# Experts' results stored from the sync engine's queue of weight loads instead of from ScalarE

## What is computed

```
def expert_block(args):
    tok_b, e = args
    xb = xpad[tok_b]
    h = jax.nn.silu(xb @ w_gate[e]) * (xb @ w_up[e])
    return h @ w_down[e]
out = out.reshape(rows, d) * buf_wt[:, None].astype(out.dtype)
y = jnp.zeros((t + 1, d), out.dtype).at[buf_tok].add(out)[:t]
```

## Time and profile before

| what | value |
|---|---|
| median of 3 runs | 1728.08 us (1727.17 to 1729.11) |
| profiled execution, its own time | 1736.61 us |
| its span in the profile | 1734.5 us |
| mean granted TensorE clock | 0.922 of 2.4 GHz |
| TensorE busy | 1468.1 us (85%) |
| ScalarE busy | 486.5 us (28%) |
| VectorE busy | 705.7 us (41%) |
| transfers | 336.88 MB |

### The profile page before, as it was taken

The page is one execution under the profiler, slowest core; times in us unless marked ns, Lnnn a source line. Parts: engine busy times, 40 slices in busy tenths (PEclk is TensorE's granted clock), DMA queues, the critical chain, the costliest instruction groups (busy, mean ns, idle before and its releaser), DMA issues.

```text
span 1734.5 us, 17917 instructions
## 1 busy us (share of the span) xinstructions
PE 1468.1 (85%) x6858; PEld 1003.7 (58%) x6858; DVE 705.7 (41%) x1297; ACT 486.5 (28%) x723; POOL 37.6 (2%) x73
## 2 busy tenths in 40 slices
PE   6999979966867767997572699998899999999976
PEld 5787766432322322333220588877788888888865
DVE  4576656101010102010003575644526666666645
ACT  5543440100000000000002522232434444444532
POOL 1000000000000000000002001000000000000000
PEclk9998998988988989998786799998999999999988
DMA  9646444996877973498774555321122121212101
GB/s 354 274 149 232 170 147 193 387 406 255 335 311 309 403 303 147 183 419 329 305 308 145 204 202 199 148 88 70 49 98 93 53 98 49 97 58 89 49 1 61
DMA packets 48139, 336.88 MB, mean 194 GB/s; under 512 B 3600, under 2 KB 3728, under 8 KB 17424
## 3 DMA queue, kind: packets, MB, share of 16 engines
q1 hardware_dynamic: 36480, 295.77, 42.9%
q0 software_dynamic: 6624, 29.89, 4.8%
q10 hardware_dynamic: 4912, 9.51, 1.5%
HBM read 312.62 MB, written 22.54 MB: 193 GB/s over the span
## 4 chain that ended last, share of the span: by engine, by line
PE 42%; ACTq 2%; DVE 2%; ACT 2%; DMA 1%; another core or an unknown queue 1%; issue 1%; POOL 0%; DVEq 0%; POOLq 0%
PE ps L290 41%; ACTq L1018 2%; PE ps L718 1%; DMA y_scratch<-gate 1%; ACT ar L860 0%; DVE b_NL L1305 0%; DMA ar<-y_scratch,rt 0%; DVE ar L1297 0%; DVE hres L1788 0%; ACT b_NH L869 0%; PE ps L296 0%; DVE ar L1971 0%; ACT ar L1085 0%; DVE ar L1256 0%
## 5 line engine op out<-in xcount | busy, mean ns | idle before, releaser
L290 PE MATMUL ps<-ring,ar 128*64 128x512 f32 x800 | 256.5, 636 | 82.3 <-ACT ar L1007 62.3
L290 PE MATMUL ps<-ar 128*64 128x512 f32 (+5 forms) x798 | 240.8, 501 | 38.8 <-ACT ar L1007 20.2
L290 PE MATMUL ps<-b_NH,b_WH 128*128 128x512 f32 x704 | 187.0, 401 | 9.7 <-DVE b_NL L1305 5.0
L290 PEld LDWEIGHTS ps<-ring,ar 128*64 128x64 f32 x800 | 77.9, 147 | 198.8 <-issue 129.0
L290 PE MATMUL ps<-b_NH,b_WL 128*128 128x512 f32 x704 | 181.6, 394 | 0.0
L1238 DVE TENSOR_TENSOR b_WL<-ring,b_WH 128x1024 fp32r<-128x1024 f32 x112 | 136.7, 1221 | 96.9 <-ACT b_WH L812 96.9
L290 PE MATMUL ps<-b_NL,b_WH 128*128 128x512 f32 x704 | 173.8, 390 | 0.0
L290 PEld LDWEIGHTS ps<-ar 128*64 128x64 f32 (+3 forms) x798 | 98.5, 167 | 127.8 <-issue 97.2
L812 ACT ACTIVATE b_WH<-ring 128x1024 fp32r<-128x1024 f32 x112 | 118.1, 1055 | 163.0 <-PE ps L290 159.8
L290 PE MATMUL ps<-spare,ar 128*64 128x512 f32 x416 | 135.2, 638 | 23.6 <-ACT ar L1007 15.1
L290 PEld LDWEIGHTS ps<-b_NH,b_WH 128*128 128x128 f32 x704 | 130.7, 191 | 38.0 <-ACT b_NH L869 10.0
(11 more groups left out here) (269 smaller groups left out, 1888.6 us busy)
## 6 DMA issues: line engine op xcount, KB each, us to landing
ring<-in_wts_dram SPq DMA_DIRECT2D x84, 2048.0 KB, 13.3
ar<-in_wts_dram SPq DMA_DIRECT2D x24, 2048.0 KB, 20.9
spare<-in_wts_dram SPq DMA_DIRECT2D x24, 2048.0 KB, 21.1
ring<-in_wmod_dram SPq DMA_DIRECT2D x24, 512.0 KB, 4.8
ar<-in_wmod_dram POOLq DMA_DIRECT2D x24, 512.0 KB, 4.1
y_scratch<-gate POOLq DMA_DIRECT2D x11, 1024.0 KB, 21.4
y_scratch<-gate ACTq DMA_DIRECT2D x22, 256.0 KB
y_scratch<-ar ACTq DMA_DIRECT2D x10, 256.0 KB
```

The lines of the kernel that those rows point to most:

```text
L290: return pe.matmul(o, l, m, start=start, stop=stop, skip_group_check=True)
```

## The change

The store of each expert's rows moves from ScalarE's instruction list to SP's, and from ScalarE's DMA queue to the queue of the weight loads. SP issues it behind the load into the slot of that expert's last panel. The store of a second block moves too, behind the load into the slot of the expert's second panel; it becomes one transfer of 2 x 64 x 512, and all waits on `ty` count 16 for a block instead of 32.

```
             act.activation(ysb[n % 3], ps[:, 5, :], ACT.Copy).then_inc(S["m_y"], 1)
-            act.wait_ge(S["m_y"], n + 1)
-            act.dma_start(y_d[n * CAP:(n + 1) * CAP, :].rearrange("t (q c) -> q t c", q=2),
-                          ysb[n % 3]).then_inc(S[f"y{n % 3}"], 16)
-
-        def store_third(u):
-
-            r = NE * CAP + CAP * u
-            for hf in range(2):
-                act.dma_start(y_d[r:r + CAP, hf * 512:(hf + 1) * 512],
-                             ysb3[64 * hf:64 * hf + 64, :]).then_inc(S["ty"], 16)
...
             act.activation(ysb3, ps[:, 1, :], ACT.Copy).then_inc(S["t_y"], 1)
-            act.wait_ge(S["t_y"], u + 1)
-            store_third(u)
...
-                    act.wait_ge(S["ty"], 32 * n)
+                    act.wait_ge(S["ty"], 16 * n)
...
-                dve.wait_ge(S["ty"], 32 * u)
+                dve.wait_ge(S["ty"], 16 * u)
...
+        def store(b, y, sem):
+
+            sp.dma_start(y_d[b * CAP:(b + 1) * CAP, :].rearrange("t (q c) -> q t c", q=2), y).then_inc(S[sem], 16)
+
         for n in range(NE):
             for m in range(3):
                 i = P_MOE + 3 * n + m + 8
...
                 if P_MOE + 3 * n + m == former[P_C0]:
                     load(P_C0)
+                if m == 1:
+                    with sp.If(third(n)):
+                        sp.wait_ge(S["t_y"], n + 1)
+                        store(NE + n, ysb3, "ty")
+            sp.wait_ge(S["m_y"], n + 1)
+            store(n, ysb[n % 3], f"y{n % 3}")
```

More of the change, by code:

```diff
@@ L1056, in scalar_program @@
                             act.wait_ge(S[v], n)
-                        act.wait_ge(S["ty"], 32 * n)
+                        act.wait_ge(S["ty"], 16 * n)
                     for v in ("t_xg", "t_sg", "t_ht", "t_y"):
                         act.sem_inc(S[v], 1)
-                    act.sem_inc(S["ty"], 32)
+                    act.sem_inc(S["ty"], 16)
                 if n:
@@ L2036, in gpsimd_program @@
                 with pool.If(n_over > j):
-                    pool.wait_ge(S["ty"], 32 * (NE + j + 1))
+                    pool.wait_ge(S["ty"], 16 * (NE + j + 1))
             pool.wait_ge(S["ovx"], 1)
@@ L2042, in gpsimd_program @@
                 pool.wait_ge(S[f"y{j}"], 16 * len(range(j, NE, 3)))
-            pool.wait_ge(S["ty"], 32 * NE)
+            pool.wait_ge(S["ty"], 16 * NE)
             pool.wait_ge(S["yzero"], 16 * 11)
@@ L2131, in sync_program @@
                     expert(0, 2).then_inc(S["v_w0"], 16)
-                    sp.wait_ge(S["t_d2"], NE + j + 1)
-                    sp.wait_ge(S["ty"], 32 * (NE + j + 1))
+                    sp.wait_ge(S["t_y"], NE + j + 1)
+                    store(2 * NE + j, ysb3, "ty")
+                    sp.wait_ge(S["ty"], 16 * (NE + j + 1))
             sp.wait_ge(S["m_d2"], NE)
@@ L2139, in sync_program @@
                 sp.wait_ge(S[f"y{j}"], 16 * len(range(j, NE, 3)))
-            sp.wait_ge(S["ty"], 32 * NE)
+            sp.wait_ge(S["ty"], 16 * NE)
             sp.dma_start(fgr, row(R_FG, 1024)).then_inc(S["fgain"], 16)
```

## The result

The changed kernel takes 1741.17 us (median of 4 runs, 1739.7 to 1742.28), the kernel before 1728.59 us beside it: 12.6 us more, a ratio of 1.007 with an interval from 1.0053 to 1.0088. It is slower, by an interval that lies wholly above 1; the changed kernel was measured in this one set. The prediction was 1727.7 us, with a range that ended at 1737.

The account below looks back on a forecast made before the run. The prediction took the two DMA engines that carry the stores as the bound. Its terms, -9.5 + 4.0 + 5.1 = -0.4 us, carried to the median of 1728.08, gave 1727.7 us, with a range from 1717 to 1737.

Parts of the forecast that it names:

- The bound: Expert loop: the two DMA engines carrying stores are the limit, 19.9 us an expert; ScalarE's hold only shows it.
- much faster: Rival, expert loop: stores spread over all sixteen engines, or the pair is not the bound; 130 us gained, 1598; chance 0.03.
- ScalarE's issues go: Expert loop: 273.6 us of work held behind ScalarE's store issues goes, and `copy_h` is no longer delayed.
- TensorE waits for landings instead: Expert loop: TensorE waits for landings instead of `copy_h`, since the bytes on the two engines stay the same.
- SP's added work costs nothing: SP's list: 34 issues at about 0.4 us, 32 branches and a 0.60 us wait, costed at nothing.
- Gain 9.5 us: First stretch, to expert 19's second block: its gather starts at 643.2, before 652.69; result 18 moves from 679.89 to 670.4.
- Loss 3.8, taken as 4 us: Block 20's `xT3` waits for block 19's store, landing 27.6 us after down projection 18; VectorE is there after 23.9.
- 5.1 us for block 20's store: Second stretch, to the last store: block 20's joined store now takes the two engines 5.14 us there, a loss.
- Sum: Whole change: -9.5 + 4.0 + 5.1 = -0.4 us.
- slower: SP is held: Rival, loop: SP is held at stores and the two engines rest 2.6 us, 29 times: 75 us, 1803; chance 0.23.
- A little faster: Rival: in one queue stores go at the pace of loads and block 20 does not wait: 1716, half 1722; chance 0.24.

Follow-up runs that it names:

- the earlier store: Changed kernel with the second block's joined 2 x 64 x 512 store, still on SP, issued ahead of the load that waits for the previous expert's down projection: 1730.23 us, 1.0016.

## Why the prediction was wrong

**The bound: right.** Two DMA engines carry loads and stores, and the loop runs at their pace. Spreading the stores shows it: some 110 us, for which the rival "much faster" had worked out 130. That rival did not come about because the change keeps the shape.

**ScalarE's issues go, TensorE waits for landings instead, SP's added work costs nothing: right, within what the runs can tell.** The kernel with the second blocks left on ScalarE isolates this, 0.9996 [0.9977, 1.0016].

**"Gain 9.5 us" in the first stretch: the step that failed.** The working compared a sum for the changed kernel with one execution of before, and that execution was late. The sum gave result 18 at 670.4, 379.5 us after the first load. The traced execution of before had it at 389.0, but the two later ones at 380.9 and 381.0. With these the gain would have been 1.5 us, the sum -1.5 + 4.0 + 5.1 = +7.6, and the forecast slower. What the changed kernel measured is 384.2: 4.8 us earlier than in the first trace of before, not 9.5, and 3.3 us later than in the other two. The term had the wrong sign. The clue was on the page: the execution was 8.5 us above the median, and I carried that difference to the result as if it lay outside the loop, when 7.5 us of it lay in the very stretch that I took a gain from (343.5 against 336.0 to result 17).

**The size of that stretch: too small by 4.7 us.** The changed kernel needs 384.2 us, not 379.5. Up projection 19, which waits for panel 58, started 2.3 us later after the first load than the sum had it, and took 9.8 us instead of 8.6. From the gather of block 19 to result 18 it took 28.3 us instead of the 27.2 of before. TensorE, changed kernel, at these places:

```profile
630.58 1.08 PE L290 MATMUL ps<-ar 128*64 128x512 f32 x1 [4.96 <-issue]
...
639.80 0.59 PE L290 MATMUL ps<-ring,ar 128*64 128x512 f32 x1
643.71 1.98 PE L290 MATMUL ps<-xhi,ar 128*64 128x512 f32 x4 [3.31 <-DVE ar L1710]
...
650.17 1.04 PE L290 MATMUL ps<-xhi,ar 128*64 128x512 f32 x4
```

After a wait a matmul takes 1.08 and 1.98 / 4 us where it later takes 0.59 and 1.04 / 4: that is the lower of the clock's two levels (granted 0.50 from 631 to 635, 1.00 from 637 to 640). The sum had this only as far as one row of before had it: its 8.6 us were read from an up projection that began with 1.08 too, but came up to speed sooner. At full clock throughout, up projection 19 takes 7.1 us in the trace below. The same place in the kernel before, profiled again; the first row is the last matmul of up projection 19:

```profile
635.26 0.59 PE L290 MATMUL ps<-ring,ar 128*64 128x512 f32 x1
643.44 1.98 PE L290 MATMUL ps<-xhi,ar 128*64 128x512 f32 x4 [7.58 <-DVE ar L1722]
```

There up projection 19 ends 7 us earlier, counted from the first load (635.85 - 290.61 = 345.2 against 640.39 - 287.84 = 352.6 us), and ScalarE's hold then gives back 4.3 of it (7.58 against 3.31 of idle time). I read this as loads that run ahead of waiting stores while these have a queue of their own, and can't in one line. The single packets in the trace of before fit it: near 412 us, with both queues waiting, each of the two engines takes a 2 KB store packet and an 8 KB load packet in turn, 0.39 us for the two. A store has 64 packets on each engine and a load 16, so at this rate a store takes 24.7 us (64 x 0.386), an estimate, and up to four loads pass meanwhile. No run tests the reading by itself. The trade came out 3 to 4 us against the change in this profile (result 17 to 18 takes 48.7 us, 44.9 before). With the earlier store it is 48.7 too, in the three other kernels whose results SP stores joined 45.4 to 47.1, and the medians of these don't show it. So how much of it is lasting stays open.

**"Loss 3.8, taken as 4 us" for block 19's store: right mechanism, short by 1.9.** The landing was predicted 27.6 us after down projection 18, and VectorE started 28.0 after. But VectorE was ready at 22.2 us, not at the 23.9 of the earlier trace rows, which makes the wait 5.8; and the matmuls behind it ran at the lower clock at first. The 1.7 us are the clock once more: where block 20's gather runs at full clock throughout (four matmuls in 1.06 to 1.08 us), VectorE is ready at 22.2, in the changed kernel and in the second trace of before; where a few of its rows take 1.5 to 2.0 us, as in the other two traces of before, it is ready at 23.9. The stretch was forecast at 44.7 us and took 46.6.

**5.1 us for block 20's store: right.** Result 19 to the gather took 5.9 us more than in the trace of before, and 4.9 and 4.8 more than in the kernels with results on SP and this store in two transfers (225.1 against 220.3 and 220.3). The round after it, with ScalarE waiting for `ty`, was forecast at some 28 us after down projection 19 and came at 747.55 - 718.62 = 28.9. The DMA engines had the load issued last to serve until 740, and then the two had the store: from 742 to 746 the share is 0.13, so the pair did not rest.

**Sum.** The forecast of the loop was 648.5 us; it took 655.9, by 4.7 + 1.9 + 0.8 = 7.4. The median of before belongs to a loop of some 639.8, not 648.9, another 9.1. Together 16.5 us against a forecast of -0.4 give the 16.1 by which the loops differ; 4.5 of them are not seen in the spans, as the changed kernel's time outside the loop was shorter in these profiles, for a reason that stays open.

**The rival "slower: SP is held": wrong, though the sign was right.** SP is held up to 15.46 us at a load, but no rest of 0.12 us an expert shows: the kernel with all results on SP and the second blocks as they were is level with before, and between 340 and 620 us no microsecond of the changed kernel has a DMA share below 0.10. The slowdown is two stores out of 34. **"A little faster": wrong**; in one queue the pair did not serve stores faster (results 0 to 17 come 18.9 us apart in the changed kernel and in the two later traces of before). Its price, 1716, also lies just outside the range that was meant to reach down to it, 1717.

**How the 12.6 us divide**, by medians whose intervals reach 2 to 4 us to either side: the shape 3 to 4, where no loads issued with it stand ahead of it; shape and place together 8 to 10 more; the place without the shape nothing that can be told (1.001), the results on SP nothing that can be told. Place and shape count together: behind the same three loads and a store, the split store let VectorE start 24.4 us after result 18, when it was all but ready, and the joined one at 28.0.

## What to carry to other kernels

Before a gain is read from one trace, hold its execution against the median: if it is several us off, find the stretch where the excess lies, or profile again, before any term uses that stretch. Where many engines wait but a DMA share of 0.13 stands beside it, look at the shape of the transfer before its issuer: moving a 2 x 64 x 512 store changed nothing, cutting it in two took 6.5% off. A store that lets someone go on belongs ahead of the loads that are issued at the same time, above all when few engines carry it.

## What the runs showed that I had not expected

An engine that issues transfers can be held for many times the cost of an issue, and the hold goes with the queue, not the engine: ScalarE 20.11 us with stores in its queue, SP 15.46 us at a load once the stores were in SP's. It vanished when the stores were spread (1.10 us for two issues on ScalarE; SP's loads 3.38 us at most with every store in their queue). No run here shows what limit the queue meets.

The kernel before scatters widely: 23 runs in one set range from 1721.0 to 1737.5 us, 12 of the kernel with the results on SP and the second blocks on ScalarE, in the same set, from 1725.0 to 1731.3. In another set its 17 runs lie closer, from 1722.5 to 1732.8. What picks its path between executions was not tried.
